# A split attention score: its second product over 64 rows instead of 128, the keys' low part kept once

## The reference, cut to what matters

```
s = jnp.einsum('bqhgd,bkhd->bhgqk', qb, kb).astype(jnp.float32) * scale      # NSA window and SWA
s = jnp.einsum('bqhgd,bhqnld->bhgqnl', qc, kg).astype(jnp.float32) * scale   # NSA selected blocks
s = jnp.einsum('brqhd,brkwhd->bhrqkw', q, k).astype(jnp.float32) + bias      # NA
```

## Time and profile before

| | us |
|---|---|
| median of 3 runs | 2685.29 |
| lowest and highest | 2681.62, 2685.42 |
| the profiled execution | 2683.39 |
| its span (first to last instruction) | 2681.2 |
| mean granted TensorE clock | 0.973 |

### The profile page before, as it was taken

How to read it: one execution, slowest core, us unless ns; L and a number is a source line. 1 busy time by engine, 2 the same in 40 slices (tenths; PEclk the granted TensorE clock), 3 DMA queues, 4 the chain that set the end, 5 groups by cost and what they waited for, 6 DMA issues and landing times. The chain is left out here.

```text
span 2681.2 us, 36597 instructions
## 1 busy us (share of the span) xinstructions
PE 2519.5 (94%) x11854; PEld 2038.9 (76%) x11854; DVE 1330.3 (50%) x2616; ACT 715.8 (27%) x1504; POOL 1772.3 (66%) x993
## 2 busy tenths in 40 slices
PE   8998889899999979899998999999999899999998
PEld 6786677588888767688886777777877777787877
DVE  6467886443342575411223566664138334751552
ACT  4305785301101263300112222222016232100002
POOL 4465455577777576577775544455779767687884
PEclk9998999999999989999999999999999999999999
DMA  7682001264563202233332311212423214233332
GB/s 262 188 232 72 1 1 39 94 206 153 176 194 94 63 17 91 74 98 94 96 100 71 102 56 57 62 56 66 108 83 71 82 50 123 79 105 91 89 104 75
DMA packets 420545, 259.73 MB, mean 97 GB/s; under 512 B 62844, under 2 KB 411513, under 8 KB 414017
## 3 DMA queue, kind: packets, MB, share of 16 engines
q1 hardware_dynamic: 395024, 199.47, 25.7%
q10 hardware_dynamic: 25393, 58.63, 6.6%
HBM read 253.86 MB, written 8.10 MB: 98 GB/s over the span
## 5 line engine op out<-in xcount | busy, mean ns | idle before, releaser
L677 POOL TENSOR_TENSOR W<-RAW,zeros 128x1024 fp32r<-128x1024 f32 (+2 forms) x349 | 668.2, 1915 | 657.8 <-PE PA L778 312.8
L684 POOL TENSOR_TENSOR W<-RAW,W 128x1024 fp32r<-128x1024 f32 (+2 forms) x355 | 849.1, 2392 | 49.2 <-ACT W L1543 19.4
L775 PE MATMUL PA<-H,W 128*128 128x512 f32 x1288 | 506.0, 393 | 7.7 <-DVEq L2412 2.3
L778 PE MATMUL PA<-H,W 128*128 128x512 f32 x1288 | 503.4, 391 | 0.0
L775 PE MATMUL PA<-A,W 128*128 128x512 f32 x944 | 373.9, 396 | 16.5 <-DVE A L2038 10.7
L778 PE MATMUL PA<-A,W 128*128 128x512 f32 x944 | 371.8, 394 | 0.0
L786 PE MATMUL PA<-H,W 128*128 128x512 f32 x1288 | 318.3, 389 | 0.0
L775 PEld LDWEIGHTS PA<-H,W 128*128 128x128 f32 x1288 | 242.3, 188 | 62.4 <-POOL W L677 7.4
L778 PEld LDWEIGHTS PA<-H,W 128*128 128x128 f32 x1288 | 242.4, 188 | 50.5 <-issue 0.5
L786 PEld LDWEIGHTS PA<-H,W 128*128 128x128 f32 x1288 | 241.7, 188 | 50.3
L786 PE MATMUL PA<-A,W 128*128 128x512 f32 x944 | 236.7, 393 | 0.0
(11 more groups left out here) (375 smaller groups left out, 3929.8 us busy)
## 6 DMA issues: line engine op xcount, KB each, us to landing
AD<-in_ada_w_dram ACTq DMA_DIRECT2D x40, 1024.0 KB, 5.1
RAW<-in_w_in_dram SPq DMA_DIRECT2D x160, 256.0 KB, 3.1
RAW<-in_mlp_w_up_dram SPq DMA_DIRECT2D x128, 256.0 KB, 3.0
RAW<-in_mlp_w_down_dram SPq DMA_DIRECT2D x128, 256.0 KB, 3.0
RAW<-in_w_up_dram SPq DMA_DIRECT2D x88, 256.0 KB, 3.1
RAW<-in_nsa_w_in_dram SPq DMA_DIRECT2D x40, 256.0 KB, 4.1
RAW<-in_w_down_dram SPq DMA_DIRECT2D x16, 384.0 KB, 3.4
RAW<-in_swa_w_in_dram SPq DMA_DIRECT2D x20, 256.0 KB, 3.3
```

What stands on the lines that cost most here:

```text
L677: e.tensor_tensor(W[0][:, s, 0:kc], RAW[:, s, 0:kc], zeros[:, 0:1].rearrange("p (a b) -> p a b", b=1).broadcast_to([P, kc, P]), ALU.add).t ...
L684: e.tensor_tensor(W[1][:, s, 0:kc], RAW[:, s, 0:kc], W[0][:, s, 0:kc].bitcast(F32), ALU.subtract).then_inc(w_split, 1)
L775: pe.matmul(PA[s][:, 0:n], W[0][:, s, k], hi, start=(k == 0), stop=False)
L778: mm = pe.matmul(PA[s][:, 0:n], W[0][:, s, k], lo, start=False, stop=False)
```

## The change

The second product takes only the near half: q_hi·k_lo over 64 rows. The term q_lo·k_lo is no longer computed. The keys' low part is written to the near half alone, so each key split on VectorE has one low instruction and not two. The high parts stay as they were, on both halves, and so do the first product, the queries' split and all waits.

```
     def split_k(dst, src, lo):
         near, far = slice(lo, lo + HD), slice(HD - lo, P - lo)
         hi = dst[0][near, :]
-        return ([(hi, src), (dst[0][far, :], src)], [(dst[1][near, :], src, hi), (dst[1][far, :], src, hi)])
+        return ([(hi, src), (dst[0][far, :], src)], [(dst[1][near, :], src, hi)])
...
-    def stacked_scores(h, keys, b, k0, k1):
-        q = QS[h % 2][:, qcols(b)]
-        return [(q, keys[0][:, k0:k1]), (q, keys[1][:, k0:k1])]
+    def stacked_scores(h, keys, lo, b, k0, k1):
+
+        near = slice(lo, lo + HD)
+        return [(QS[h % 2][:, qcols(b)], keys[0][:, k0:k1]), (QS[h % 2][near, qcols(b)], keys[1][near, k0:k1])]
```

More of the change, by code:

```diff
@@ L544, in plan_nsa @@
                     need=[("q", h), ("k", n, g)], need_v=("v", n, g), head=h, first=n == 0, out=None, rows=P, keys=[(b + 1) * P for b in range(NT)],
-                    at=[0] * NT, scores=[stacked_scores(h, KK[m], b, 0, (b + 1) * P) for b in range(NT)],
+                    at=[0] * NT, scores=[stacked_scores(h, KK[m], lo, b, 0, (b + 1) * P) for b in range(NT)],
                     values=[(VV[1 if n else g % 2 * 2][:, t, :], x, t, t, NT) for t in range(NT) for x in range(2)],
@@ L571, in plan_swa @@
                 keys=[(b + 1 - starts[b]) * P for b in range(NT)], at=starts,
-                scores=[stacked_scores(h, KK[g], b, starts[b] * P, (b + 1) * P) for b in range(NT)],
+                scores=[stacked_scores(h, KK[g], lo, b, starts[b] * P, (b + 1) * P) for b in range(NT)],
                 values=[(VS[:, t, 0:P], 0, t, a, z) for t in range(NT)
@@ L590, in plan_na @@
                 need=[("q", h), ("k", h)], need_v=("v", h), head=h, first=True, out=("halves", OF[lo:lo + HD, h // 2, :]), rows=P,
-                keys=[S] * NT, at=[0] * NT, scores=[stacked_scores(h, KK[h % 2], b, 0, S) for b in range(NT)],
+                keys=[S] * NT, at=[0] * NT, scores=[stacked_scores(h, KK[h % 2], lo, b, 0, S) for b in range(NT)],
                 values=[(VV[h % 2][:, t, :], x, t, a, a + 2) for a in (0, 2) for t in range(NT) for x in range(2)],
```

## The result

The changed kernel takes 2727.06 us (median of 4, 2719.1 to 2734.23) against 2685.36 us before: ratio 1.016, 95% interval 1.0142 to 1.0179, so 41.7 us slower. The profiled execution is the fastest of the four, 2719.1 us with a span of 2716.9: 35.7 us above the span of before.

What follows compares the result with a forecast made beforehand. TensorE, 94% busy, was taken as the bound, nearly tied with other engines in the changed stretches. Form changes beyond idle time +26.8 us, low parts −2.8, sum +24.0, gave 2708 us; range 2688 to 2742.

Steps and rivals of the forecast that it cites:

- The direction and the mechanism: Stacked units: slower, since halving rows saves TensorE nothing and the array's form changes twice a unit.
- The price of a change: At each form change, 0.15 to 0.20 us on TensorE; 80 us in all over 224 units.
- The subtraction of idle time: NSA, SWA, NA: TensorE's added time less its idle 31.7, 12.9 and 8.6 us gives +26.8 us.
- The two errors that I let cancel: In that subtraction: idle time at stage starts cannot be filled; overlapping records hide some idle time. No net size.
- rival A: Mainly NSA: slower and the clock falls too, 19 us more there, about 2730 us; chance 15%.
- the forecast's 13.1: NSA: 44.8 us of added TensorE time less 31.7 us idle, so 13.1 us longer.
- 1.4 for the start: NSA's start: two low parts standing bare before scores go, 0.69 us each.
- the forecast's own 2694 to 2722: Whole kernel: 2694 to 2722 us for a price per unit between 0.30 and 0.45; chance 65%.
- the stated range: Whole kernel: 2688 to 2742 us, leaving out the faster rival and the slow tail beyond 2742.
- The low parts: VectorE: 18 fewer key instructions, 12.4 us; four at stage starts give −2.8 us, the other 14 nothing.
- the ring: Engines that bound a stretch together; in NSA TensorE, VectorE and ScalarE, busy 171.3, 172.1 and 163.7 of 203 us.

Runs made afterwards that it cites:

- experiment 1: Changed kernel's 64-row second products, but the keys' low part still made on both halves as in the kernel before: 2734.52 us, ratio 1.0189.
- experiment 8: Kernel before, with the second product over 96 rows for heads whose queries' high part lies in partitions 0 to 63: 2683.89 us, one run.
- experiment 10: Kernel before, with NSA's compressed scores run over 128 rows: 2679.37 us, ratio 0.9983.
- the twin: Kernel before, with the 128-row second product made three times instead of once in every stacked unit: 2713.94 us, ratio 1.0102.
- experiment 9: Changed kernel, with its 64-row product made twice in a row: 2804.04 us, one run.
- experiment 2: Kernel before, products still over 128 rows, keys' low part on the near half alone and far half zeroed at first use: 2685.18 us, ratio 0.9997.
- experiment 3: Changed kernel, with the 64-row product placed first of the two: 2743.81 us, ratio 1.0215.
- The full form: Kernel before, with NSA's compressed scores over 128 rows and compressed values over 96: 2676.68 us, ratio 0.9967.

## Why the prediction was right, and where it fell short

*The direction and the mechanism* were right: no product went, a 64-row load was no shorter, and the form changed twice a unit. The page shows it, and experiments 1, 8 and 10 tie it to the rows.

*The price of a change* was right where it could be read. I had 0.43 us in place of 0.23 between a 512-column product and the next. Here the first product's record is at 301.25 (it truly starts at about 301.30, its load having begun at 301.19), the 64-row load at 301.62, the product truly 0.11 later: 0.43. In NA, from a unit's first product to the second panel product behind it, the way grew from 0.70 to 1.09 us, by 0.39 where 0.40 was forecast.

*The subtraction of idle time* was the weak step: it gave +26.8 us, and the three stretches grew by 37.8. It read PE's idle time from windows with the stages' ends in them. NA had 3.3 us idle between its first and last score, not 8.6, and grew by 8.6, not by 4.2. For NSA it took 31.7 us as fillable; the twin, with some 40 us added, let 17 through, so about 23 fitted in. The two errors that I let cancel did not: SWA absorbed more than thought (4.3 in place of 9.5), NSA and NA less. With the idle times between first and last score (27.4, 10.1 and 3.3) the same subtraction gives 17.4 + 12.3 + 9.5 = 39.2, near the 37.8 measured, but partly by luck: NSA would be 7.5 too short and SWA 8.0 too long.

*The clock* was rival A, at 15%, and not in the sum. It came true in NSA in part: 0.86, where A had 0.82 and a price of 19 us. The reason given against it, that TensorE's idle gaps get shorter, failed: they did get shorter, and the clock fell. What it cost is known only within bounds. The twin leaves 8 us for 36 us of half level, 0.2 us for each. The four timed runs of the changed kernel differ by 15.1 us and by 0.006 in clock, 2 × 0.006 × 2720 = 33 us of half level, 0.46 for each, and experiment 9 gives 0.44. So of NSA's 24.9 us some 7 to 14 are clock, by estimate. The remaining 11 to 18 stand against the forecast's 13.1 less 1.4 for the start. The whole came out at 2727, near A's 2730, and above the forecast's own 2694 to 2722: the stated range holds it only because that range took in rival A. The forecast had less than 60% of the loss, 24 us of 41.7.

*The low parts* were taken as 2.8 us, all at the stages' starts; the other 14 instructions were put at nothing, since TensorE would be the slowest member. At NSA's start the term fits: one low part of 0.68 us stands before the first score in place of 1.38. In NA the zero was wrong: experiment 1's window is 101.0 − 97.3 = 3.7 us longer than the changed kernel's, at a clock of 0.96 against 0.97, which is worth about 1. In SWA the difference is 1.1 to 1.7 (79.4 against 78.3 and 77.7), in part clock too. In NSA nothing can be read: 221.2 against 222.3, but at 0.88 against 0.86. Here is experiment 1's NA:

```profile
2024.90:2125.90 101.00, 99.41 (x466) 72.30 (x466) 77.76 (x160) 61.53 (x132) 81.25 (x44) 0.96 0.26 54
```

*What the Trainium skill says* (TensorEngine Tiling (Array Packing), Key Properties: a change of mode drains TensorE) agrees with the trace at 64 and 31 rows against 128: a load 0.1 us behind the end of the streaming. Experiment 8 shows that 96 against 128 is no such change.

## What to carry to other kernels

Halving the rows of a product saves nothing on TensorE and, between full-height neighbours, costs 0.15 to 0.20 us at each border: look for small row counts in the form column (here 64 and 31) and for loads that start later than the product before them, under "issue". Pad with zeros to 96 or 128 rows, where that costs no more columns; here it took 7 us off (13 together with experiment 2's edit) a kernel in which the opposite had cost 42. Read idle time only between the first and the last instruction of the ring, and price the clock on its own when products change shape.

## What the runs showed of the hardware that was not expected

In NSA the granted clock did not go with how full TensorE was. PE was busier in the changed kernel than before (96% against 86%) at a lower clock, 0.86 against 0.92; with the 64-row product twice it was 99% busy at 0.67; with two more 128-row products it was 94% busy at 0.94. Between the changed kernel and the one with the product twice, the number of form changes is the same, so there, in the one run made, it was the added 64-row products, and not emptying, that the lower clock went with. How far emptying plays a part in the changed kernel itself was not told apart.

The rows of the products do not decide the clock by themselves either. The same two products in the other order took it from 0.86 to 0.80 (experiment 3). The same change moved it by 0.01 in SWA and NA. The full form, with fewer products of few rows than the kernel before, stood at 0.90. And in experiment 9 units of one kind ran for 195 us at the half level and then for 99.6 us at the full one, with TensorE 99% busy in both. What lets the level rise or fall is not shown by these runs. The scatter of the times does not settle it: four runs of the changed kernel lie within 15 us and four of experiment 1 within 33, but four of the change in NSA alone within 4 and four of the twin within 11.
